# Sample top-k of a hybrid decoder step: one row of 1056 scores, or four quarter rows merged

## The chip, the cores and the metric

The kernel runs on one core of one Trainium2 chip as one program. The metric is device time in microseconds from start to end. Of five engines, TensorE (PE) multiplies, VectorE (DVE) and ScalarE (ACT) work on vectors, GpSimd (POOL) does side work and SyncE (SP) issues most DMAs. All wait for each other by semaphores.

## The reference

A two-layer decoder trunk processes 256 prompt tokens and 32 sample tokens (8 sequences of 4) with shared weights. Layer 0 has, between two SwiGLU halves, a sparse attention beside RWKV-7. The sample part of that attention is what changes; its definition, cut:

```python
def dsa_sample(q, k, v, qi, ki, wi, ck, cv, cki, page_table):
    ki_all = jnp.concatenate([ki_past, ki], axis=1)          # 1024 past keys from 8 pages, then the new ones
    isc = indexer_scores(qi, ki_all, wi)                     # sum over 16 heads of relu(qi . ki) * wi
    isc = jnp.where(adm[None], isc, -jnp.inf)
    vals, sel = lax.top_k(isc, topk)                         # topk = 256
    ...
    kg = jnp.where(is_past, ck[phys, off].astype(k.dtype), gather_rows(k, new_i))
    vg = jnp.where(is_past, cv[phys, off].astype(v.dtype), gather_rows(v, new_i))
    return sparse_attend(q, kg, vg, jnp.isfinite(vals))      # softmax over the 256 chosen keys
```

The prompt part is the same with 256 keys and the best 64 of them. The kernel does not gather: it turns the choice into a mask of 0 and -1e30 and adds it to dense scores.

## The kernel before, in words

Everything around the change is `dsa_stage`, in the profile from 364 to about 569 us. The rest of the program (four feed-forward stages, projections, RWKV, retention and mLSTM) stands as it is, and starts after this stage ends on all engines.

Each engine has its own list of instructions, in the order in which the code is written; semaphores set who waits.

- SP loads parameters (L1351), then the cache pages by the page table: `load` (L1353) reads eight page numbers into registers and issues eight DMAs of 256 KB. Keys of sequences 0 and 1 go first, those of 2 and 3 once `is_sum` is 12 (the index keys are read), then values of 0 and 1, keys of 4 to 7, values of 2 to 7. Each later load waits until TensorE is done with the slot (`kv_used`).
- Index scores: for the prompt L1395, L1547 and L1620. For the samples TensorE runs 12 steps (4 groups of two sequences by 3 chunks of 512, 512 and 32 keys): a product with the index keys (L1419), a ReLU on ACT (L1554), and `weigh` (L1407), which sums the heads into 32 rows in banks 5 to 7.
- VectorE picks the prompt's top 64 (L1631, L1635), copies the sample scores into `iss` and `wks` (L1666 to L1670, 32 rows of 1056), then goes through the eight prompt heads. `head(h)` (L1650, L1651) takes the row maximum, which ACT's exponential (L1570) waits for; `norm(h)` (L1656) gives the reciprocal sum to ACT; `out` (L1660) stores a pair of heads. Between two heads stand four calls of `top_eight` (L1676, L1678): take the eight largest of each of the 32 rows, and strike them out. 32 calls give 256.
- TensorE for each head h: scores (L1474 product, L1476 adds the prompt's mask), transposes of head h-1 (L1434, waits for ACT's norm, which stands after the exponential of head h), values of head h-2 (L1445), and after each odd head the dense key scores of two sequences (L1462).
- After the last head VectorE makes the mask (L1692, L1693; semaphore `ms_done`), TensorE spreads it (L1495), and softmax, transposes (L1505) and values (L1524, L1526) of the samples follow.

```python
for i in range(h * (KS // 8) // 8, (h + 1) * (KS // 8) // 8):
    top_eight(i)
```

## Time and profile before

| | |
|---|---|
| three timed runs | 1709.56, 1713.64 (median), 1715.57 us |
| profiled execution | 1715.16 us, span of the core 1713.3 us |
| busy in the span | PE 1516.6 (89%), DVE 1158.1 (68%), ACT 311.5 (18%), POOL 304.1 (18%) us |
| DMA | 232.77 MB, mean 136 GB/s |

How to read it: busy shares are averages over stages with different limits; the changed stage is about an eighth of the span and is read from its own rows. The profile follows the chain that ended last only through the final stages, so the path through this stage is put together here from the timelines of VectorE, TensorE and SP and from who waited for whom.

### The profile page before, as it was taken

To read this page: it belongs to the slowest core of one execution; us is meant where nothing else is said; L and a number is where in the kernel's file an instruction comes from. 1 tells how busy PE (TensorE), PEld (TensorE's weight loads), DVE (VectorE), ACT (ScalarE), POOL (GpSimd) and SP (SyncE) were. 2 spreads that over 40 slices of the span, in tenths; PEclk is the share of its full clock that TensorE was granted. 3 is DMA by queue.
4 is the path that set the end of the run, shared out by engine and by line. 5 is a ranking of instruction groups with operands and counts; after the bars stand their busy time and mean duration, and the time that the engine had idled before them with its cause. 6 is when DMAs were issued, how large, how long until landed. Compare 5 with 4: busy or idle time off the path is not lost. (4 is left out here: it accounts for less than half of the span.)

```text
span 1713.3 us, 28197 instructions
## 1 busy us (share of the span) xinstructions
PE 1516.6 (89%) x11288; PEld 1346.1 (79%) x11288; DVE 1158.1 (68%) x1396; ACT 311.5 (18%) x599; POOL 304.1 (18%) x270
## 2 busy tenths in 40 slices
PE   6999999986778568668999989999998986999997
PEld 6999989952333258468999989999895664899997
DVE  6877857639782473478876868768573447687764
ACT  2111020022111222123111021110201202321110
POOL 3333120000000000024332133321100000343310
PEclk9999999987768779879999999999999566999999
DMA  7442716533745200044443634426142003444242
GB/s 272 148 171 90 243 47 217 196 109 130 240 148 175 74 1 3 29 175 190 169 171 117 217 110 172 168 89 240 67 159 99 5 25 126 166 172 171 98 135 96
DMA packets 62963, 232.77 MB, mean 136 GB/s; under 512 B 9271, under 2 KB 19165, under 8 KB 45717
## 3 DMA queue, kind: packets, MB, share of 16 engines
q1 hardware_dynamic: 51578, 225.81, 37.4%
q10 hardware_dynamic: 11290, 5.63, 1.1%
q8 instruction: 68, 1.11, 0.3%
q14 instruction: 27, 0.21, 0.0%
HBM read 225.31 MB, written 6.10 MB: 135 GB/s over the span
## 5 line engine op out<-in xcount | busy, mean ns | idle before, releaser
L185 PE MATMUL psum<-x_hi_r,pair_hi 128*128 128x288 f32 x1744 | 520.7, 299 | 36.0 <-DVE ring_r L180 36.0
L187 PE MATMUL psum<-x_hi_r,ring_r 128*128 128x288 f32 x1744 | 519.5, 298 | 0.0
L186 PE MATMUL psum<-x_lo_r,pair_hi 128*128 128x288 f32 x1616 | 478.7, 296 | 0.0
L185 PEld LDWEIGHTS psum<-x_hi_r,pair_hi 128*128 128x128 f32 x1744 | 332.4, 191 | 39.5 <-DVE ring_r L180 39.1
L187 PEld LDWEIGHTS psum<-x_hi_r,ring_r 128*128 128x128 f32 x1744 | 331.8, 190 | 0.0
L180 DVE TENSOR_TENSOR ring_r<-ring,pair_hi 128x2048 fp32r<-128x2048 f32 x127 | 327.2, 2577 | 4.3
L186 PEld LDWEIGHTS psum<-x_lo_r,pair_hi 128*128 128x128 f32 x1616 | 306.4, 190 | 0.4
L185 PE MATMUL psum<-hidden_hi_r,down_hi 128*128 128x288 f32 x704 | 208.5, 296 | 0.0
L186 PE MATMUL psum<-hidden_r,down_hi 128*128 128x288 f32 x704 | 207.9, 295 | 0.0
L187 PE MATMUL psum<-hidden_hi_r,down_r 128*128 128x288 f32 x704 | 207.2, 294 | 0.0
L171 DVE CAST pair_hi<-ring 128x2048 fp32r<-128x2048 f32 x127 | 159.4, 1255 | 34.7 <-DMA ring<-in_w_gu 17.3
L614 POOL TENSOR_TENSOR hidden<-silu,up 128x288 f32 x88 | 128.4, 1459 | 148.9 <-ACT silu L543 147.3
L187 PEld LDWEIGHTS psum<-hidden_hi_r,down_r 128*128 128x128 f32 x704 | 132.6, 188 | 0.0
L186 PEld LDWEIGHTS psum<-hidden_r,down_hi 128*128 128x128 f32 x704 | 132.2, 188 | 0.0
L185 PEld LDWEIGHTS psum<-hidden_hi_r,down_hi 128*128 128x128 f32 x704 | 132.0, 188 | 0.0
L180 DVE TENSOR_TENSOR down_r<-down,down_hi 128x1408 fp32r<-128x1408 f32 x64 | 116.6, 1822 | 2.2
L543 ACT ACTIVATE silu<-gate 128x288 f32<-128x288 f32 x88 | 39.2, 446 | 425.5 <-DVE gate L558 425.5
L180 POOL TENSOR_TENSOR hidden_r<-hidden,hidden_hi_r x88 | 74.1, 842 | 212.5 <-DVE hidden_hi_r L171 212.5
L558 DVE TENSOR_TENSOR gate<-psum,rstd 128x288 f32<-128x288 f32 x88 | 40.0, 455 | 95.4 <-PE psum L187 95.3
L171 DVE CAST down_hi<-down 128x1408 fp32r<-128x1408 f32 x64 | 62.1, 970 | 49.3 <-PE psum L187 29.0
L229 PE MATMUL psum<-x_hi_r,pair_hi 128*128 128x288 f32 x192 | 54.5, 304 | 17.4 <-DVE ring_r L180 12.0
L622 POOL TENSOR_TENSOR ysq<-ysq,y 128x288 f32<-128x288 f32 x24 | 30.6, 1277 | 181.0 <-ACT y L549 181.0
(488 smaller groups left out, 1930.0 us busy)
## 6 DMA issues: line engine op xcount, KB each, us to landing
ring<-in_w_gu SPq DMA_DIRECT2D x88, 1024.0 KB, 4.8
down<-in_w_down SPq DMA_DIRECT2D x64, 704.0 KB, 4.4
ring<-in_w_ab SPq DMA_DIRECT2D x18, 1024.0 KB, 5.2
ring<-in_w_cd SPq DMA_DIRECT2D x13, 1024.0 KB, 4.8
ring<-in_cache_k SPq DMA_DIRECT2D x32, 256.0 KB, 4.2
index_keys<-in_cache_k SPq DMA_DIRECT2D x32, 256.0 KB, 4.1
index_keys<-in_cache_i ACTq DMA_DIRECT2D x64, 64.0 KB, 2.7
eight_pages_ds<-in_cache_v SPq DMA_DIRECT2D x16, 256.0 KB, 4.3
```

Of the source, the lines that this page charges most:

```text
L171: return dve.tensor_copy(hi, a)
L180: return eng.tensor_tensor(lo, a, hi.bitcast(F32), ALU.subtract)
L185: pe.matmul(out, w_hi, x_hi, start=start, stop=False)
L186: pe.matmul(out, w_hi, x_lo, start=False, stop=False)
L187: return pe.matmul(out, w_lo, x_hi, start=False, stop=stop)
L229: pe.matmul(out, c.whi[:, s, half, k], c.xhi[:, k], start=(k == 0), stop=False)
L543: act.activation(silu[:, b], gate[:, b], ACT.Silu).then_inc(silu_done, 1)
L558: dve.tensor_tensor(gate[:, b], c.banks[bank][:, 0:NT], c.rstd[:, :], ALU.mult).then_inc(gate_scaled, 1)
L614: pool.tensor_tensor(h, silu[:, b], up[:, b], ALU.mult).then_inc(c.hidden_raw, 1)
L622: pool.tensor_tensor(ysq[:, :], ysq[:, :], y2[:, n % 2], ALU.add).then_inc(ysq_added, 1)
```

## The change

The 1056 scores of each sample row are cut into four quarters of 264 (256 past keys and 8 of the 32 new ones), and the quarters stand below each other in 128 partitions. `weigh` writes them so into one bank. `wq` is the copy on which the rounds run; quarters 1 and 3 are multiplied by -1 through a column of ±1 beside the mask (`nmask[:, 8:9]`), so their rounds bring up the smallest of the original values. 33 rounds of `top_eight` write a sorted row of 264 into `sq`. POOL issues DMAs that bring the scores back into `iss` (32 rows of 1056) and a sorted quarter beside its neighbour. `merge_quarters` takes the 256 largest of quarters 0 and 1, and of 2 and 3, and sorts them by eight levels of pairwise maximum and minimum; one more DMA puts the second list beside the first, and `select` finds the 256th value, marks what is above it, and of the equal ones as many as are missing, in order. The rounds are spread over the heads by `ROUNDS` as 6, 6, 5, 5, 6, 5, 0, 0. A second parameter tile `nmask32` is loaded, and SP queues the values of sequence 1 right behind the keys of sequences 0 and 1.

```diff
+QW = KS + 8
+ROUNDS = (0, 6, 12, 17, 22, 28, 33, 33, 33)
...
-        iss, wks = sb("iss", [NS, KEYS]), sb("wks", [NS, KEYS])
-        t8s = sb("t8s", [NS, 8])
+        iss, rank = sb("iss", [NS, KEYS]), sb("rank", [NS, KEYS])
+        above = ymix[0:NS, 4:8].rearrange("p a t -> p (a t)")[:, 0:KEYS]
+        quarters = z[:, 10:16].rearrange("p a t -> p (a t)")
+        iq, wq, sq = (quarters[:, i * QW:(i + 1) * QW] for i in range(3))
+        moved, pa_, pb_ = (quarters[:, 3 * QW + i * KS:3 * QW + (i + 1) * KS] for i in range(3))
+        n_above, n_equal, kth = (sb(n, [NS, 1]) for n in ("n_above", "n_equal", "kth"))
...
             for b in range(2):
                 load("cache_k", b, KEY_SLOTS[b], None)
+            load("cache_v", 1, VALUE_SLOTS[1], None)
             for b in range(2, 4):
                 load("cache_k", b, KEY_SLOTS[b], (S["is_sum"], 12))
-            for b in range(2):
-                load("cache_v", b, VALUE_SLOTS[b], (S["is_used"], 12) if b == 0 else None)
+            load("cache_v", 0, VALUE_SLOTS[0], (S["is_used"], 12))
             for b in range(4, NB):
                 load("cache_k", b, KEY_SLOTS[b], (S["kv_used"], b // 2 - 1))
             for b in range(2, NB):
...
+            pool.wait_ge(S["is_out"], 2)
+            for s in range(4):
+                pool.dma_start(iss[:, s * KS:(s + 1) * KS], iq[quarter(s), 0:KS]).then_inc(S["q_moved"], 16)
+                pool.dma_start(iss[:, PAST + s * 8:PAST + s * 8 + 8], iq[quarter(s), KS:QW]).then_inc(S["q_moved"], 16)
+            pool.wait_ge(S["ts_max"], QW // 8)
+            for s in (0, 2):
+                pool.dma_start(moved[quarter(s), :], sq[quarter(s + 1), 8:QW]).then_inc(S["q_moved"], 16)
+            pool.wait_ge(S["ts_max"], QW // 8 + 1)
+            pool.dma_start(moved[quarter(0), :], pa_[quarter(2), :]).then_inc(S["q_moved"], 16)
...
                 pe.wait_ge(S["is_rel"], n + 1)
-                pe.matmul(B[5 + ch][0:NS, 0:w], wsel[:, g], rel[:, n % 3, 0:w], start=(g == 0), stop=(g == 3)).then_inc(S["is_used"], 1)
+                if ch < 2:
+                    for e in range(2):
+                        mm = pe.matmul(B[5][quarter(2 * ch + e), 0:KS], wsel[:, g], rel[:, n % 3, e * KS:(e + 1) * KS],
+                                       start=(g == 0), stop=(g == 3), skip_group_check=True)
+                else:
+                    for s in range(4):
+                        mm = pe.matmul(B[5][quarter(s), KS:QW], wsel[:, g], rel[:, n % 3, 8 * s:8 * s + 8],
+                                       start=False, stop=(g == 3), skip_group_check=True)
+                mm.then_inc(S["is_used"], 1)
...
-            for ch, (c0, w) in enumerate(CHUNKS):
-                dve.wait_ge(S["is_used"], 10 + ch)
-                if ch < 2:
-                    dve.tensor_copy(iss[:, c0:c0 + w], B[5 + ch][0:NS, 0:w]).then_inc(S["is_out"], 1)
-                else:
-                    dve.tensor_tensor(iss[:, c0:c0 + w], B[5 + ch][0:NS, 0:w], nmask[:, :], ALU.add).then_inc(S["is_out"], 1)
-            dve.wait_ge(S["is_out"], 3)
-            ln(dve.tensor_copy(wks[:, :], iss[:, :]))
+            dve.wait_ge(S["is_used"], 12)
+            dve.wait_ge(S["mp_done"], 1)
+            dve.tensor_copy(iq[:, 0:KS], B[5][:, 0:KS]).then_inc(S["is_out"], 1)
+            dve.tensor_tensor(iq[:, KS:QW], B[5][:, KS:QW], nmask[:, 0:8], ALU.add).then_inc(S["is_out"], 1)
+            dve.wait_ge(S["is_out"], 2)
+            ln(dve.tensor_scalar(wq, iq, nmask[:, 8:9], None, ALU.mult))
 
             def top_eight(i):
 
                 if i:
                     dve.wait_ge(S["ts_rep"], i)
-                dve.max(t8s[:, :], wks[:, :]).then_inc(S["ts_max"], 1)
-                dve.wait_ge(S["ts_max"], i + 1)
-                dve.match_replace(out=wks[:, :], in_to_replace=t8s[:, :], in_values=wks[:, :], imm_value=TAKEN).then_inc(S["ts_rep"], 1)
+                dve.max(sq[:, 8 * i:8 * i + 8], wq).then_inc(S["ts_max"], 1)
+                if i < QW // 8 - 1:
+                    dve.wait_ge(S["ts_max"], i + 1)
+                    dve.match_replace(out=wq, in_to_replace=sq[:, 8 * i:8 * i + 8], in_values=wq, imm_value=TAKEN).then_inc(S["ts_rep"], 1)
+
+            def merge_quarters():
+
+                dve.wait_ge(S["ts_max"], QW // 8)
+                dve.wait_ge(S["q_moved"], 160)
+                dve.scalar_tensor_tensor(pa_[quarter(0)], moved[quarter(0)], -1.0, sq[quarter(0), 0:KS], ALU.mult, ALU.max)
+                ln(dve.scalar_tensor_tensor(pa_[quarter(2)], sq[quarter(2), 0:KS], -1.0, moved[quarter(2)], ALU.mult, ALU.min))
+                a, b = pa_, pb_
+                d = KS // 2
+                while d >= 1:
+                    av, bv = (x.rearrange("p (m e d) -> p m e d", e=2, d=d) for x in (a, b))
+                    dve.tensor_tensor(bv[0:96, :, 0], av[0:96, :, 0], av[0:96, :, 1], ALU.max)
+                    last = dve.tensor_tensor(bv[0:96, :, 1], av[0:96, :, 0], av[0:96, :, 1], ALU.min)
+                    if d == 1:
+                        last.then_inc(S["ts_max"], 1)
+                    else:
+                        ln(last)
+                    a, b = b, a
+                    d //= 2
+
+            def select():
+
+                dve.wait_ge(S["q_moved"], 176)
+                ln(dve.scalar_tensor_tensor(pb_[quarter(0)], moved[quarter(0)], -1.0, pa_[quarter(0)], ALU.mult, ALU.max))
+                ln(dve.tensor_reduce(kth[:, :], pb_[quarter(0)], AX_X, ALU.min))
+                ln(dve.tensor_scalar(above, iss[:, :], kth[:, 0:1], None, ALU.is_gt))
+                dve.tensor_reduce(n_above[:, :], above, AX_X, ALU.add)
+                ln(dve.tensor_scalar(iss[:, :], iss[:, :], kth[:, 0:1], None, ALU.is_equal))
+                dve.tensor_scalar(n_equal[:, :], n_above[:, :], -1.0, float(KS), ALU.mult, ALU.add)
+                ln(dve.tensor_tensor_scan(rank[:, :], c.ones[0:NS, 0:1].to_broadcast([NS, KEYS]), iss[:, :], 0.0, ALU.mult, ALU.add))
+                ln(dve.scalar_tensor_tensor(rank[:, :], rank[:, :], n_equal[:, 0:1], iss[:, :], ALU.is_le, ALU.mult))
+                ln(dve.tensor_tensor(rank[:, :], rank[:, :], above, ALU.add))
+                ln(dve.tensor_scalar(iss[:, :], rank[:, :], -NEG, NEG, ALU.mult, ALU.add))
+                dve.tensor_tensor(iss[:, PAST:KEYS], iss[:, PAST:KEYS], nmask32[:, :], ALU.add).then_inc(S["ms_done"], 1)
 
             for h in range(8):
                 head(h)
@@ -1683,14 +1743,14 @@
                     norm(h - 1)
                 if h >= 4 and h % 2 == 0:
                     out(h // 2 - 2)
-                for i in range(h * (KS // 8) // 8, (h + 1) * (KS // 8) // 8):
+                for i in range(ROUNDS[h], ROUNDS[h + 1]):
                     top_eight(i)
+                if h == 6:
+                    merge_quarters()
             norm(7)
+            select()
             out(2)
             out(3)
-            dve.wait_ge(S["ts_rep"], KS // 8)
-            ln(dve.tensor_scalar(iss[:, :], wks[:, :], -2.0e38, NEG, ALU.is_gt, ALU.mult))
-            dve.tensor_tensor(iss[:, PAST:KEYS], iss[:, PAST:KEYS], nmask[:, :], ALU.add).then_inc(S["ms_done"], 1)
             for g in range(2):
```

VectorE before, from the last rounds behind the eighth head to the mask (`t8s_ds` holds the eight maxima, `wks_ds` the copy that is struck out; L1656 is `norm`, L1660 `out`):

```order
L1650 TENSOR_REDUCE mx_ds<-psum 128x2 [waits sp_sum_ds]
L1651 TENSOR_SCALAR nb_ds<-mx_ds 128x2 [waits chain_dve]
L1656 RECIPROCAL ri_ds<-rs_ds 128x2 [waits sp_exp_ds]
L1676 MAX t8s_ds<-wks_ds 32x8 [waits ts_rep_ds]
L1678 MATCH_REPLACE wks_ds<-t8s_ds,wks_ds 32x1056 [waits ts_max_ds]
...
L1656 RECIPROCAL ri_ds<-rs_ds 128x2 [waits sp_exp_ds]
L1660 COPY ymix<-psum 128x256 [waits op_sum_ds] x2
L1692 TENSOR_SCALAR iss_ds<-wks_ds 32x1056 [waits ts_rep_ds]
L1693 TENSOR_TENSOR iss_ds<-iss_ds,nmask_ds 32x32 [waits chain_dve]
```

And after, the same place (L1677 and L1678 are `head`, L1683 `norm`, L1687 `out`, L1728 to L1738 `select`; `z` is the tile that now holds the quarters):

```order
L1677 TENSOR_REDUCE mx_ds<-psum 128x2 [waits sp_sum_ds]
L1678 TENSOR_SCALAR nb_ds<-mx_ds 128x2 [waits chain_dve]
L1683 RECIPROCAL ri_ds<-rs_ds 128x2 [waits sp_exp_ds] x2
L1728 SCALAR_TENSOR_TENSOR z<-z 32x256 [waits q_moved_ds]
L1729 TENSOR_REDUCE kth_ds<-z 32x1 [waits chain_dve]
L1730 TENSOR_SCALAR ymix<-iss_ds,kth_ds 32x1056 [waits chain_dve]
...
L1737 TENSOR_SCALAR iss_ds<-rank_ds 32x1056 [waits chain_dve]
L1738 TENSOR_TENSOR iss_ds<-iss_ds,nmask_ds 32x32 [waits chain_dve]
L1687 COPY ymix<-psum 128x256 [waits op_sum_ds] x2
```

The four rounds between the last two reciprocals are gone; the selection stands behind them and ahead of the last two stores, and waits for POOL's last DMA.

VectorE after, between the seventh head and the eighth (L1701 is the last maximum of `top_eight`, L1710 to L1717 `merge_quarters`):

```order
L1701 MAX z<-z 128x8 [waits ts_rep_ds]
L1677 TENSOR_REDUCE mx_ds<-psum 128x2 [waits sp_sum_ds]
L1678 TENSOR_SCALAR nb_ds<-mx_ds 128x2 [waits chain_dve]
L1683 RECIPROCAL ri_ds<-rs_ds 128x2 [waits sp_exp_ds]
L1687 COPY ymix<-psum 128x256 [waits op_sum_ds]
L1710 SCALAR_TENSOR_TENSOR z<-z 32x256 [waits q_moved_ds,ts_max_ds]
L1711 SCALAR_TENSOR_TENSOR z<-z 32x256
L1716 TENSOR_TENSOR z<-z 96x128 [waits chain_dve]
L1717 TENSOR_TENSOR z<-z 96x128
```

The last round ends ahead of the seventh head; the merge, of which the first of eight levels is shown, stands ahead of the eighth head's maximum and waits for POOL's first ten DMAs.

TensorE, the first steps of the sample index scores, before (L1419 is the product with the keys, L1407 `weigh`):

```order
L1419 MATMUL psum<-index_keys,qi_ds 64x512 x3
L1407 MATMUL psum<-down,wsel_ds 32x512 [waits is_rel_ds]
L1419 MATMUL psum<-z,qi_ds 64x32 x2
L1407 MATMUL psum<-down,wsel_ds 32x512 [waits is_rel_ds]
L1419 MATMUL psum<-index_keys,qi_ds 64x512 [waits is_rel_ds,index_keys_landed]
```

And after (L1446 the product, L1428 and L1432 `weigh`):

```order
L1446 MATMUL psum<-index_keys,qi_ds 64x512 x3
L1428 MATMUL psum<-down,wsel_ds 32x256 [waits is_rel_ds]
L1428 MATMUL psum<-down,wsel_ds 32x256
L1446 MATMUL psum<-z,qi_ds 64x32 x2
L1428 MATMUL psum<-down,wsel_ds 32x256 [waits is_rel_ds]
L1428 MATMUL psum<-down,wsel_ds 32x256
L1446 MATMUL psum<-index_keys,qi_ds 64x512 [waits is_rel_ds,index_keys_landed]
L1446 MATMUL psum<-index_keys,qi_ds 64x512
L1432 MATMUL psum<-down,wsel_ds 32x8 [waits is_rel_ds]
L1432 MATMUL psum<-down,wsel_ds 32x8 x3
```

Each product of 512 columns is now two of 256 that go to different column groups of 32, and each of 32 columns is four of 8.

## Rows read from the trace of the kernel before

**Rows 1.** Waits, 335 to 560 us: us in total, times, longest.
```profile
ACT x_hi L1570 <- DVE nb_ds L1651: 61.3, 8, 12.3
DVE mx_ds L1650 <- PE psum L1476: 13.2, 4, 4.9
```

**Rows 2.** Tiles t8s_ds, iss_ds: ns min/median/max, first, last start us.
```profile
L1676 DVE MAX8 t8s_ds<-wks_ds x32: 1227/1249/1249, 412.5 to 512.5; 32x8 f32<-32x1056 f32 x32
L1678 DVE MATCH_VALUE_LOAD wks_ds<-t8s_ds,wks_ds x32: 79/79/79, 413.8 to 513.8; 32x8 f32 x32
L1678 DVE MATCH_REPLACE8 wks_ds<-t8s_ds,wks_ds x32: 1229/1230/1232, 413.9 to 513.9; 32x1056 f32<-32x1056 f32 x32
...
L1692 DVE TENSOR_SCALAR iss_ds<-wks_ds x1: 686/686/686, 520.2 to 520.2; 32x1056 f32<-32x1056 f32 x1
```

**Rows 3.** Timeline of VectorE: start us, us, engine, line, [idle before].
```profile
411.74 0.69 DVE L1650 TENSOR_REDUCE mx_ds<-psum 128x2 f32<-128x512 f32 x1 [0.63 <-PE psum L1476]
...
422.93 0.67 DVE L1650 TENSOR_REDUCE mx_ds<-psum 128x2 f32<-128x512 f32 x1
...
437.29 0.69 DVE L1650 TENSOR_REDUCE mx_ds<-psum 128x2 f32<-128x512 f32 x1 [3.06 <-PE psum L1476]
...
492.23 0.69 DVE L1650 TENSOR_REDUCE mx_ds<-psum 128x2 f32<-128x512 f32 x1 [4.64 <-PE psum L1476]
...
503.82 0.67 DVE L1650 TENSOR_REDUCE mx_ds<-psum 128x2 f32<-128x512 f32 x1
```

**Rows 4.** VectorE's groups by line and shape: busy us, mean ns | idle before.
```profile
L1620 DVE SCALAR_TENSOR_TENSOR ymix<-down,wip_ds,ymix 128x256 f32<-128x256 f32 x32 | 15.4, 484 | 3.6 <-ACT down L1547 1.6
...
L1635 DVE MATCH_REPLACE8 z<-t_ds,z 128x256 f32<-128x256 f32 x16 | 6.4, 407 | 0.0
...
L1631 DVE MAX8 t_ds<-z 128x8 f32<-128x256 f32 x16 | 5.9, 412 | 0.0
...
L880 DVE TENSOR_TENSOR_SCAN D_rk<-seg_rk,D_rk 128x288 f32<-128x288 f32 x4 | 2.7, 737 | 0.0
...
L1701 DVE TENSOR_REDUCE mxs_ds<-down 128x1 f32<-128x1056 f32 x2 | 2.5, 1253 | 0.1
```

**Rows 5.** Timeline of TensorE: start us, us, engine, line, [idle before].
```profile
402.80 1.05 PE L1407 MATMUL psum<-down,wsel_ds 128*32 128x512 f32 x2
...
409.44 1.13 PE L1474 MATMUL psum<-z 64*128 64x256 f32 x4
...
499.97 2.07 PE L1476 MATMUL psum<-z,ident 128*128 128x256 f32 x4
...
509.53 7.71 PE L1462 MATMUL psum<-index_keys,qz_ds 128*32 128x512 f32 x32
...
518.01 1.84 PE L1445 MATMUL psum<-x_hi,vtok 128*64 128x256 f32 x8
...
521.18 2.38 PE L1495 MATMUL psum<-iss_ds,bsel_ds 32*128 32x512 f32 x6 [1.33 <-DVE iss_ds L1693]
...
542.68 7.06 PE L1524 MATMUL psum<-ring,x_lo 128*32 128x512 f32 x32
```

**Rows 6.** Stretches of TensorE: us, busy (x), granted clock, DMA share, GB/s.
```profile
496.00:502.00 6.00, 6.00 (x13) 0.50 0.70 236
510.00:518.00 8.00, 8.00 (x52) 0.94 0.00 0
```

**Rows 7.** Waits of the DMA queue SP, 335 to 560 us, as rows 1.
```profile
SPq L1359 <- PE psum L1462: 20.5, 3, 10.2
SPq L1359 <- PE psum L1419: 19.2, 1, 19.2
```

**Rows 8.** Timeline of the DMA queue SP: start us, us, line, DMAs issued.
```profile
429.44 0.85 SPq L1359 DMA_DIRECT2D two_pages_ds<-in_cache_v  x2
435.26 3.95 SPq L1359 DMA_DIRECT2D eight_pages_ds<-in_cache_v  x8
```

More of the change, by code:

```diff
@@ L1284, in dsa_stage @@
         "ip_sum", "ip_rel", "ip_acc", "is_sum", "is_rel", "is_used", "is_out",
-        "tp_max", "tp_rep", "mp_done", "ts_max", "ts_rep", "ms_done",
+        "tp_max", "tp_rep", "mp_done", "q_moved", "ts_max", "ts_rep", "ms_done",
         "sp_sum", "ri_done", "nb_done", "sp_exp", "pn_done", "pt_sum", "pt_out", "op_sum", "op_out",
@@ L1294, in dsa_stage @@
         cmask = sb("cmask", [P, 2, TP])
-        nmask = sb("nmask", [NS, NS])
+        nmask, nmask32 = sb("nmask", [P, 9]), sb("nmask32", [NS, NS])
         esel = sb("esel", [16, P])
@@ L1345, in half, with quarter @@
             return slice(u * 64, u * 64 + 64)
+        def quarter(s):
+            return slice(s * NS, s * NS + NS)
         @block.sync
         def _(sp):
-            for dst, src in ((kidg[:, :], "kidg"), (cmask[:, :, :], "cmask"), (nmask[:, :], "nmask"), (esel[:, :], "esel"),
+            for dst, src in ((kidg[:, :], "kidg"), (cmask[:, :, :], "cmask"), (nmask[:, :], "nmask"), (nmask32[:, :], "nmask32"), (esel[:, :], "esel"),
                              (wmask[:, :, :], "wmask"), (bsel[:, :, :], "bsel")):
@@ L1383, in _ @@
             pe.matmul(B[0][:, 0:NT], c.half_ones[:, :], kisq[:, :], start=True, stop=True).then_inc(S["ki_sum"], 1)
-            pe.wait_ge(S["par_loaded"], 96)
+            pe.wait_ge(S["par_loaded"], 112)
             for t in range(2):
@@ L1451, in key_scores @@
                     pe.wait_ge(S["qz_done"], 1)
-                    pe.wait_ge(S["is_out"], 3)
+                    pe.wait_ge(S["is_out"], 2)
                 if b0 == 4:
@@ L1598, in ln @@
                 c.link(dve, "dve", ins)
-            dve.wait_ge(S["par_loaded"], 96)
+            dve.wait_ge(S["par_loaded"], 112)
             dve.wait_ge(S["ki_sd"], 1)
@@ L2449, in lay_out_dsa @@
     t, s = np.arange(NS)[:, None], np.arange(NS)[None]
-    m["nmask"] = np.where((s <= t) & (s // TS == t // TS), 0, NEG).astype(np.float32)
+    m["nmask32"] = np.where((s <= t) & (s // TS == t // TS), 0, NEG).astype(np.float32)
+    m["nmask"] = np.concatenate([m["nmask32"].reshape(NS, 4, 8).transpose(1, 0, 2).reshape(P, 8), 1.0 - 2.0 * (np.arange(P)[:, None] // NS % 2)], 1).astype(np.float32)
     row = np.arange(P)
```

## The prediction, made before the changed kernel was run

> **What bounds the stage now.** I began with who waited for whom around the attention stage, because the profile's chain of waits covers only the end of the program. Two rows matter: ScalarE's exponentials waited 61.3 us in eight waits for VectorE's head maxima, and VectorE's head maxima waited 13.2 us in four for TensorE's scores [rows 1]. So VectorE is late at most heads, TensorE at some. The timeline of VectorE shows which [rows 3]. From head 0 (411.74) to head 1 (422.93) it has no idle time: 11.19 us, almost all of it top-k rounds. Head 2 comes at 437.29 after 3.06 us idle, so there TensorE is last. From head 6 (492.23, after 4.64 idle) to head 7 (503.82) are 11.59 us without idle again. The pattern alternates: the steps 0-1, 2-3, 4-5 and 6-7 are VectorE's, the steps 1-2, 3-4 and 5-6, which hold the dense key scores, are TensorE's.
>
> I then asked in each VectorE step when TensorE would have been ready. For head 7 its mask product starts at 499.97 and takes 2.07, so it ends at 502.04 [rows 5]; the head starts at 503.82 [rows 3]. That small difference is the point of this forecast: TensorE stands close behind VectorE.
>
> **Cost of a round.** Before, 32 rounds of 1.249 + 0.079 + 1.230 = 2.56 us by their medians [rows 2]; with the gaps, about 0.07 in the step from head 0 to 1 ((11.19 - 0.80 for the head's own work) / 4 = 2.60), I take 2.62, 84 us in all. After, 33 rounds of 264 elements. The same two operations with 256 elements took 0.412 and 0.407 [rows 4]; between 256 and 1056 elements the slope is 1.04 ns an element, so 264 give 0.42 and 0.415. With the value load 0.08 and the gaps 0.07 a round is 0.985 us, 33 are 32.5 us. VectorE thus gets rid of about 52 us, but the time falls only by what TensorE lets through:
>
> 1. *Weighing of the sample scores.* A product of 512 columns took 1.05 us in two passes, 0.52 a pass [rows 5]. Where neighbouring products go to other column groups, 32 passes of 512 took 7.06, 0.22 each [rows 5]. The change makes two products of 256 columns in different column groups of each of eight such ones: four passes of half the length, 4 x 0.11 = 0.44, say 0.55. That saves 0.45 to 0.5 each, 3.9 in all; the four small products become four of 8 columns each, +0.1 each. So TensorE starts head 0's scores 3.4 earlier than at 409.44 [rows 5], less 0.5 for the added parameter load ahead of the stage (eight DMA issues took 3.95, 0.49 each [rows 8]), on which both engines wait. VectorE copies 264 columns instead of 1056 meanwhile, under these scores. It is itself busy with the prompt's top-k until about 407, which holds the gain at about **3.0**. Bounds: 3.4 if nothing binds; -0.7 (a loss) if the passes do not overlap and the added ones cost 0.2 us.
> 2. *Head 0 to 1.* TensorE has these scores early. VectorE needs 0.8 + 6 x 0.985 = 6.7 instead of 11.19: **4.5**. Bounds of a round 0.9 and 1.1 give 5.0 and 3.8.
> 3. *Heads 2-3, 4-5 and 6-7.* VectorE would need 7.3 (head, reciprocal, store and six rounds, or the merge), TensorE 502.1 - 492.23 = 9.9. So 11.59 becomes 9.9: 1.7 each, three times **5.1**. TensorE is late next.
> 4. *Heads 1-2, 3-4, 5-6.* TensorE's already, with VectorE idle: **0**.
> 5. *Merge.* Two operations of 256 at 0.484 [rows 4]; eight levels of two of 128 elements, each 0.484 less 128 x 1.04 ns = 0.35, plus 0.07 for the link: 1.0 + 6.2 = 7.1 us, from 1.5 us after head 6 to 8.6. Hidden by TensorE's 9.9; if strided access doubled the levels, head 7 would be 4.9 late.
> 6. *End.* The mask product started at 521.18, after 1.33 idle, while the last values ended at 518.01 + 1.84 = 519.85 [rows 5]. With the mask ready earlier it starts then: **1.3**. The mask must be ready: `select` begins at head 7 + 1.9 and has one operation of 256 (0.48), a reduction of 256 (0.42 by the slope from 1253 [rows 4]), three scalar passes of 1056 at 0.686 [rows 2], three more of at most 1.25, a scan of 1056 elements (288 took 0.737 [rows 4]: 2.7), three small ones and nine gaps, 1.2: 10.6 us, so it ends at head 7 + 12.5. The `out` copy behind it is needed by values 6 at 518.01 - 503.82 = head 7 + 14.2. Hidden with 1.3 to spare.
> 7. *Values of sequence 1 earlier.* The load takes about 9 us of SP (5.0 for the page numbers between 430.29 and 435.26, 3.95 to issue [rows 8]) and moves into a wait of 19.2 us for the last index-key product [rows 7]. The keys of sequences 4 and 5 can then be issued 9 us earlier, but SP waited 20.5 us in three waits for TensorE's key scores anyway [rows 7], and no key score waited for pages in this trace. **0**, from -0.5 to 1.
> 8. *POOL's eleven DMAs.* POOL had nothing else there. The first ten have until the merge, some 10 us after the last round. The eleventh must land by head 7 + 14.2 - 0.4 - 10.6 = head 7 + 3.2, that is 13.1 after head 6, and is released at 8.6: 4.5 us. Page loads of 256 KB share the DMA engines; this one is 32 KB. **0**, at worst 3 to 4 us.
>
> All behind the mask (softmax, transposes, values, last pages) follows TensorE's steps as before and only moves. Sum: 3.0 + 4.5 + 5.1 + 1.3 = 13.9 us. The profiled execution took 1715.16; 1715.16 - 13.9 = 1701.3. It was 1.5 above the median 1713.64 of the runs, so I forecast 1713.64 - 13.9 = 1699.7, said as **1700**. What can be told from no change is 0.3%, 5.1 us.
>
> **Rivals.**
> *TensorE's clock stays up (1692).* In 496 to 502 TensorE was busy all 6.00 us at a granted clock of 0.50, its level of 1.2 GHz, after waiting; in 510 to 518, key scores, it had 0.94, nearly 2.4 GHz [rows 6]. After the change its wait ahead of each odd head's transposes is 1.7 us shorter (item 3). If that keeps 2.4 GHz, a VectorE step needs 6.9 on TensorE and 7.3 on VectorE: 2.6 more, three times, 8 us. Against it: the other wait, for ScalarE's result behind each even head, stays as it is, and the stretch at 0.50 stands behind that one.
>
> *TensorE's clock does not come back (slower).* Its place is the four blocks of key scores. One took 7.71 us [rows 5], at 0.94; the same work at 0.50 takes 14.5, so 6.8 more. Four such blocks cost 27 us: 1699.7 + 27 = 1727. It decides from the third block on (two cost 13.6, the gain). Against it: the clock came up in this block after a longer wait than it will have now.
>
> *Weighing does not overlap.* Then item 1 gives -0.7 instead of 3.0: 1703.4. The 0.22 of a pass speaks against it; there both neighbours have their own data in SBUF, here they share weights.
>
> *POOL's transfers are late.* A last DMA that takes L us after its release costs L - 4.5: at 8 us 1703, at 14 us 1709. The rows for it are missing: POOL issues no DMA in this stage before. The Trainium skill, "SBUF — State Buffer", section "SBUF: two separate sides", says that a DMA issued from GpSimd cannot have its descriptors written while VectorE runs an operation in a two-port mode, and its next section tells of 620 ns becoming 3100. By that rule 2.5 us would be added, still inside the 4.5, so the sum would stay at 1700; no row here shows it. VectorE is idle behind the merge, so there is little to hold POOL up.
>
> *The steps hide nothing new (no change).* If TensorE's chain grew by what VectorE gives up in items 2, 3 and 6, for instance by page loads in its way, 1709 to 1714 would be left. No key score waited for pages, so little speaks for it.
>
> **How the numbers follow.** Forecast 1700 (its own range 1696 to 1704): 0.58. Clock stays up: 0.14. No overlap in weighing: 0.10. POOL late: 0.09, of which 0.02 ends within 0.3%. No change: 0.05. Slower by the clock: 0.04. Faster by over 0.3% (below 1708.5): 0.58 + 0.14 + 0.10 + 0.07 = 0.89; same 0.07; slower 0.04. The range from 1689 to 1708 takes in the clock rival and the two small losses and leaves out the last two and the far end of the first.
>
> **What would show it.** Right: rounds of about 0.98 us; 6.7 us from head 0 to 1 and 9.9 from 2 to 3, 4 to 5 and 6 to 7, each with VectorE now waiting for TensorE's scores (L1503); head 0 about 3 us earlier; merge of 7 and selection of 11 us or less, followed by no wait on TensorE; the mask product right behind the last values. Wrong: a head that waits for POOL's DMAs; a clock of 1.0 between even and odd heads, or of 0.5 in the key scores; products of 256 columns that take 0.5 us each; a mask product that waits for `select`.

## The result, and the profile after

The changed kernel took **1683.8 us** (median of 4 runs, 1682.84 to 1693.94) against 1713.7: ratio 0.984, 95% interval 0.980 to 0.988. That is 29.9 us faster where 13.9 were forecast, and outside the range of 1689 to 1708. Run twice more beside the experiments it gave 1689.0 and 1685.0; over all 14 of its runs the median is 1685.9, over all 67 of the kernel before 1713.3, so the change is worth about 27 us. Its profiled execution had a span of 1681.1 (before: 1713.3), its mean granted clock was 0.928 (before: 0.912).

All stretches below are read from the traces. "Start to head 0" runs from the stage's first product of the index keys' sums to VectorE's first head maximum, "end" from head 7 to the mask product (L1495 before, L1522 after), the last row from POOL's first memset of the RWKV stage to POOL's first copy behind it, in the output projection; all in us:

| stretch | before | after | change | forecast |
|---|---|---|---|---|
| start to head 0 | 47.07 | 43.53 | -3.5 | -3.0 |
| head 0-1 | 11.19 | 6.68 | -4.5 | -4.5 |
| 2-3, 4-5, 6-7 | 11.26, 11.59, 11.59 | 7.96, 7.07, 7.96 | -11.4 | -5.1 |
| 1-2, 3-4, 5-6 | 14.36, 16.15, 15.94 | 14.81, 13.86, 15.49 | -2.3 | 0 |
| end | 17.36 | 14.14 | -3.2 | -1.3 |
| RWKV stage behind it (unchanged code) | 175.75 | 169.32 | -6.4 | 0 |

The rest of the program gives -0.8, the whole -32.2. The timeline of VectorE in the changed kernel (start us, us, engine, line, idle before it and its releaser), where [rows 3] stood:

```profile
407.12 0.69 DVE L1677 TENSOR_REDUCE mx_ds<-psum 128x2 f32<-128x512 f32 x1 [0.29 <-PE psum L1503]
...
413.80 0.68 DVE L1677 TENSOR_REDUCE mx_ds<-psum 128x2 f32<-128x512 f32 x1
...
428.61 0.69 DVE L1677 TENSOR_REDUCE mx_ds<-psum 128x2 f32<-128x512 f32 x1 [8.00 <-PE psum L1503]
...
436.57 0.69 DVE L1677 TENSOR_REDUCE mx_ds<-psum 128x2 f32<-128x512 f32 x1 [2.14 <-PE psum L1503]
...
450.43 0.69 DVE L1677 TENSOR_REDUCE mx_ds<-psum 128x2 f32<-128x512 f32 x1 [8.03 <-PE psum L1503]
...
457.50 0.68 DVE L1677 TENSOR_REDUCE mx_ds<-psum 128x2 f32<-128x512 f32 x1
```

VectorE waits for scores at six heads now instead of four, and not at head 5 (457.50), where it was still forecast to wait. The waits of the stage, where [rows 1] stood, say the same (us in total, times, longest):

```profile
ACT x_hi L1597 <- DVE nb_ds L1678: 45.9, 8, 12.3
...
DVE mx_ds L1677 <- PE psum L1503: 30.4, 6, 10.2
```

The rounds, from the tile view (ns min/median/max, first and last start), where [rows 2] stood:

```profile
L1701 DVE MAX8 z<-z x33: 414/436/436, 407.9 to 462.3; 128x8 f32<-128x264 f32 x33
...
L1704 DVE MATCH_VALUE_LOAD z<-z x32: 92/92/93, 408.4 to 461.8; 128x8 f32 x32
L1704 DVE MATCH_REPLACE8 z<-z x32: 416/417/419, 408.5 to 461.9; 128x264 f32<-128x264 f32 x32
...
L1716 DVE TENSOR_TENSOR z<-z x8: 286/286/290, 475.1 to 478.7; 96x128 f32<-96x128 f32 x8
```

0.436 + 0.092 + 0.417 and the gaps make a round of 1.00 us (MAX8 at 407.92, the next at 408.92), against 0.985 forecast. Merge and selection, again VectorE's timeline:

```profile
474.19 0.40 DVE L1710 SCALAR_TENSOR_TENSOR z<-z 32x256 f32<-32x256 f32 x1
...
478.94 0.28 DVE L1717 TENSOR_TENSOR z<-z 96x128 f32<-96x128 f32 x1
480.95 0.69 DVE L1677 TENSOR_REDUCE mx_ds<-psum 128x2 f32<-128x512 f32 x1 [1.73 <-PE psum L1503]
...
483.01 0.39 DVE L1728 SCALAR_TENSOR_TENSOR z<-z 32x256 f32<-32x256 f32 x1
...
492.43 0.18 DVE L1738 TENSOR_TENSOR iss_ds<-iss_ds,nmask_ds 32x32 f32<-32x32 f32 x1
```

The merge is over 1.73 us before head 7, the selection takes 9.6 us and is over 2.4 us before TensorE has finished the last values (at 495.00). Now TensorE's timeline, where [rows 5] stood. It is here that the trace departs from the forecast:

```profile
393.59 0.63 PE L1428 MATMUL psum<-down,wsel_ds 128*32 128x256 f32 x4
...
431.40 1.11 PE L1461 MATMUL psum<-ident,x_hi 128*128 128x128 f32 x4 [2.83 <-ACT x_hi L1591]
432.44 1.97 PE L1472 MATMUL psum<-x_hi,vtok 128*64 128x256 f32 x4
434.34 1.13 PE L1501 MATMUL psum<-z 64*128 64x256 f32 x4
435.40 1.13 PE L1503 MATMUL psum<-z,ident 128*128 128x256 f32 x4
...
439.36 0.66 PE L1461 MATMUL psum<-ident,x_hi 128*128 128x128 f32 x4 [2.83 <-ACT x_hi L1591]
439.95 1.08 PE L1472 MATMUL psum<-x_hi,vtok 128*64 128x256 f32 x4
440.96 7.06 PE L1489 MATMUL psum<-index_keys,qz_ds 128*32 128x512 f32 x32
...
493.17 1.83 PE L1472 MATMUL psum<-x_hi,vtok 128*64 128x256 f32 x8
495.09 2.35 PE L1522 MATMUL psum<-iss_ds,bsel_ds 32*128 32x512 f32 x6
```

Behind head 2 (431.40) the four transposes take 1.11 us and the four products of the values 1.97, the speed of 1.2 GHz. The scores of head 3 behind them (L1501, L1503) take 1.13 each, the speed of 2.4 GHz, where such a product took 2.07 in the step that the forecast used [rows 5]. That alone makes head 3 some 2 us earlier. Behind head 3 (439.36), after a wait of the same 2.83 us, transposes and values take 0.66 and 1.08: 2.4 GHz, which stays through the key scores. The stretches (us, busy, granted clock, DMA share, GB/s) put the clock beside it, where [rows 6] stood:

```profile
430.00:437.00 7.00, 5.13 (x16) 0.76 0.74 221
437.00:444.00 7.00, 4.64 (x24) 1.00 0.69 231
444.00:451.00 7.00, 6.39 (x44) 1.00 0.63 223
```

POOL's DMAs, from the view of DMA issues (KB each, median us from issue to landing), and POOL's timeline:

```profile
iss_ds<-z POOLq DMA_DIRECT2D x4, 32.0 KB, 5.0
z<-z POOLq DMA_DIRECT2D x3, 32.0 KB, 2.5
```

```profile
479.51 0.50 POOL L1397 DMA_DIRECT2D z<-z  x1 [15.46 <-DVE z L1717]
```

Nothing waited for them.

### The profile page after: what moved, and what is told of

It is laid out like the page before. It is cut to its first block and busy times, and to the rows that moved or that the text cites. A ratio compares the mean times of both kernels' runs of the same rounds, so it can differ in the third digit from the quotient of the medians.

```text
span 1681.1 us, 28318 instructions
## 1 busy us (share of the span) xinstructions
PE 1494.1 (89%) x11328; PEld 1337.2 (80%) x11328; DVE 1117.7 (66%) x1423; ACT 310.8 (18%) x599; POOL 309.0 (18%) x281
## 3 DMA queue, kind: packets, MB, share of 16 engines
q8 instruction: 68, 1.11, 0.3%
```

## The experiments

Twelve runs were made: eight further kernels, the changed kernel twice more, and e2 and the kernel before once more each. The theory under test: the part that the forecast missed is TensorE's clock, not work. Rival theories: the earlier loads of values did it; or the changed kernel's stage merely came at a lucky moment.

**Both ends of the clock taken away.** To the changed kernel, small products whose results are never read were added where TensorE waits for ScalarE (behind `mm.then_inc(S["sp_sum"], 1)`), so that it idles less; the kernel before got the same with 24, 12 or 5 of them:

```diff
+for _ in range(0 if h == 0 else 14 if h == 1 else 5 if h % 2 else 5):
+    pe.matmul(B[2 if h < 2 else (h + 1) % 2][:, 0:TP], c.ident[:, :], mp[:, 0], start=True, stop=True, skip_group_check=True)
```

> The changed kernel with products whose result nobody reads (identity by a prompt mask tile, 128x256), issued by TensorE behind the scores of each head from the second on: 14 behind head 1's, 5 behind each later one, so that it is busy where it would wait. Theory A: the remaining stretches at 1.2 GHz go: 1-2 13.4 instead of 14.8 us, 2-3 and 6-7 about 7.1 instead of 8.0, 5-6 13.9 instead of 15.5: 4 to 5 us less than the changed kernel, near 1679. Theory B: the products do not make anything faster, 1684 or a few us more where they delay the transposes.

> The kernel before with the same kind of unread products: 24 behind head 1's scores, 12 behind later odd heads', 5 behind even ones'. VectorE's rounds stay as long as before. Theory A: VectorE's steps stay at 11.2 to 11.6 us, but 3-4 and 5-6 fall from 16.1 to about 13.9 and 1-2 from 14.4 to 13.4, about 5 to 6 us less in all (1708). Theory B: no change, 1713.7, or slower.

e2: 1682.87 us (1681.24 to 1685.35); e3: 1706.12 (1704.19 to 1715.09), ratio to before 0.996, 0.994 to 0.998. In the traces the stretch from head 0 to the mask product is 81.64 us in e2 and 103.06 in e3, against 87.97 and 109.44 without filling. So filling is worth 6.4 us in the kernel before, and 6.3 against this trace of the changed one. With the clock up in both the change takes 21.4 us from this stretch: 4.5 in step 0-1, 14.1 in the steps 2-3, 4-5 and 6-7, 2.8 at the end, and nothing in the other steps. Without filling it was 21.5 in this trace, but 14.9 and 19.3 in two later ones (e5, e10); that 21.5 and 21.4 agree is chance. The forecast for this stretch, 10.9 us, set the new work against the old clock. In time, e2 is only 1 us below the first runs of the changed kernel and 3 below all 14: its RWKV stage came out longer (174.71 against 169.32), on which more below.

**One part at a time.** e1: the kernel before, with rounds over the first 264 scores only; it leaves the other three quarters out of the choice, and nothing else moved. e8: the kernel before with only the weighing in quarters; it copies the first quarter four times and so leaves the other three out as well.

```diff
-dve.max(t8s[:, :], wks[:, :]).then_inc(S["ts_max"], 1)
+dve.max(t8s[:, :], wks[:, 0:264]).then_inc(S["ts_max"], 1)
...
-dve.match_replace(out=wks[:, :], in_to_replace=t8s[:, :], in_values=wks[:, :], imm_value=TAKEN).then_inc(S["ts_rep"], 1)
+dve.match_replace(out=wks[:, 0:264], in_to_replace=t8s[:, :], in_values=wks[:, 0:264], imm_value=TAKEN).then_inc(S["ts_rep"], 1)
```

> The kernel before, with one edit: the 32 rounds read and strike only the first 264 of the 1056 scores (the other three quarters of the scores are left out of the choice). It has no quartered weighing, no merge, no selection, no moves by POOL and the old order of loads, so it isolates the length of the rounds. Theory A (TensorE's clock stays up once its waits for VectorE are short): 0-1 takes 4.9 us, 2-3 and 6-7 about 8.0, 4-5 7.1 to 8, 3-4 13.9 instead of 16.15, the end 15.4; from head 0 to the mask product 88 us against 109.4 before, about 21 us faster in that stretch. Theory B (only the VectorE steps shrink and TensorE's own speed stays as it was): 0-1 4.9, the three other VectorE steps 9.9, TensorE's steps 14.4 to 16.1 as before: about 11 us faster.

e1: 1699.45 (1698.04 to 1701.42), ratio 0.990, 0.987 to 0.993: 14 us, half of the whole. Head 0 to mask 95.61, between the 88 of theory A and the 98.4 of theory B, so neither was met. Its trace shows what is missing. After the second wait of 2.83 us its clock was still at 1.2 GHz, and the key scores began there (TensorE's timeline):

```profile
441.81 1.12 PE L1434 MATMUL psum<-ident,x_hi 128*128 128x128 f32 x4 [2.83 <-ACT x_hi L1564]
442.86 1.97 PE L1445 MATMUL psum<-x_hi,vtok 128*64 128x256 f32 x4
444.76 7.82 PE L1462 MATMUL psum<-index_keys,qz_ds 128*32 128x512 f32 x32
```

For e8 the products of `weigh` are those of the change, and `iss` is filled from them:

```diff
+dve.wait_ge(S["is_used"], 12)
+for c0 in (0, 256, 512, 768):
+    dve.tensor_copy(iss[:, c0:c0 + 256], B[5][0:NS, 0:256])
...
```

> The kernel before with only the quartered weighing: two products of 256 columns, or four of 8, in different column groups of one bank. VectorE copies the first quarter of the scores four times instead of all four quarters (three quarters of the scores are left out). If the passes overlap, the last weighing ends about 3.5 us earlier and head 0 comes 2.3 us earlier than before: about 1711. If they do not, head 0 comes 0.5 us later than before. The steps from head 0 on as before, 11.2, 14.4, 11.3, 16.1, 11.6, 15.9, 11.6.

e8: 1713.66 (1704.13 to 1716.37), ratio 0.9993, 0.998 to 1.001: no gain. Head 0 came 2.4 us earlier, so the halves do overlap, but steps 1-2 and 3-4 took 15.47 and 16.71 instead of 14.36 and 16.15, because the key scores ran more of their time at the lower clock. The first block of them, TensorE's timeline:

```profile
423.37 1.11 PE L1447 MATMUL psum<-ident,x_hi 128*128 128x128 f32 x4 [12.96 <-ACT x_hi L1577]
424.41 9.25 PE L1475 MATMUL psum<-ring,qz_ds 128*32 128x512 f32 x32
```

32 products in 9.25 us, where the same block took 8.14 in the kernel before and such a block takes 7.06 at the full clock. A gain ahead of a wait can be lost to the clock behind it.

**Is it the length of the waits?** e4 gives the changed kernel its long steps back: VectorE has six more reductions at heads 2, 4 and 6.

```diff
+if h in (2, 4, 6):
+    for _ in range(6):
+        ln(dve.tensor_reduce(t8[:, 0, 0:1], cmask[:, :, :].rearrange("p a t -> p (a t)"), AX_X, ALU.max))
```

> The changed kernel with six reductions of 128x512 that nobody reads behind the rounds of heads 2, 4 and 6 (behind the merge at head 6), 0.72 us each, 4.3 a head: VectorE's steps 2-3, 4-5, 6-7 take 10.3 to 11.4 us again and TensorE waits as long as before. Theory A: TensorE's clock falls again: 3-4 goes back from 13.9 to 16.1, the end from 14.1 to about 16, beside the 2.4, 4.3 and 2.7 us of the lengthened steps: 13 to 14 us slower than the changed kernel, near 1697. Theory B: only the lengthened steps, 9.4 us, near 1693, and 3-4 stays at 13.9.

e4: 1702.55 (1698.78 to 1704.39), ratio 0.992, 0.989 to 0.995. Head 0 to mask 103.13, 15.2 more than in the changed kernel's trace; the lengthened steps themselves hold 8.9 of that (10.05, 11.39, 10.46 instead of 7.96, 7.07, 7.96), the other 6.3 lie in steps 3-4 and 5-6 and the end, whose work is unchanged. Against e5 and e10 that second part is 3.4 and 5.6. e5, below, lost as much with nothing lengthened, so e4 fits the theory without proving it; and of the waits behind the odd heads it made only one much longer (3.04, 6.22 and 3.45 us, where the kernel before had 4.22, 4.54 and 4.54). Its transposes and values run at 1.2 GHz behind every head from 2 on:

```profile
469.28 1.11 PE L1461 MATMUL psum<-ident,x_hi 128*128 128x128 f32 x4 [6.22 <-ACT x_hi L1591]
470.32 1.97 PE L1472 MATMUL psum<-x_hi,vtok 128*64 128x256 f32 x4
472.22 8.22 PE L1489 MATMUL psum<-ring,qz_ds 128*32 128x512 f32 x32
```

**Is it the moment?** The changed kernel twice more, and once with its prompt top-k, and with it the heads, some 2 us later:

```diff
+for _ in range(3):
+    ln(dve.tensor_reduce(mx[:, 0, 0:1], cmask[:, :, :].rearrange("p a t -> p (a t)"), AX_X, ALU.max))
```

> The changed kernel once more, unchanged, for a second trace and more times. Theory A (how fast TensorE's clock comes and goes depends on the lengths of its waits alone): the steps from head 0 on repeat to 0.1 us (6.68, 14.81, 7.96, 13.86, 7.07, 15.49, 7.96, end 14.14) and the RWKV stage repeats 169.3. Theory C (after waits of 2.8 us the clock falls or stays by where in time they lie, so that it differs between executions): the even-odd steps lie between 6.7 and 10, the odd-even ones between 13.8 and 16.8, their sum differs by several us, and the RWKV stage lies somewhere between 169 and 176.

> The changed kernel with three reductions of 128x512 that nobody reads ahead of the prompt's top-k, so that everything from head 0 on comes about 2.1 us later and nothing behind is changed. Theory A: all steps as in the changed kernel, 2.1 us slower (about 1686). Theory C: the steps come out otherwise, with stretches at 1.2 GHz in other heads, and the time changes by something else than 2.1 us, anywhere from -3 to +10.

> The changed kernel unchanged, a third trace and more times beside the filled one. Theory C: head 0 to the mask product between 82 and 99 us, the steps that differ from the other two traces are those with stretches at 1.2 GHz; steps 0-1 and 4-5 (VectorE's) at 6.7 and 7.1 always. Median of its runs between 1684 and 1690.

e5: 1688.96 (1683.75 to 1689.6), ratio 0.984, 0.982 to 0.987; e10: 1685.03 (1683.36 to 1691.61); e6: 1684.47 (1683.12 to 1691.31), not to be told from them. Head 0 to mask in the traces: 94.59 in e5, 90.11 in e10, 87.95 in e6. The same program, then, with waits of the same length, keeps the clock at one head and loses it at another. In e5, behind head 3, where the first trace had 0.66 and 1.08:

```profile
441.25 1.12 PE L1461 MATMUL psum<-ident,x_hi 128*128 128x128 f32 x4 [2.83 <-ACT x_hi L1591]
442.30 1.97 PE L1472 MATMUL psum<-x_hi,vtok 128*64 128x256 f32 x4
444.20 7.19 PE L1489 MATMUL psum<-index_keys,qz_ds 128*32 128x512 f32 x32
```

```profile
430.00:437.00 7.00, 5.60 (x14) 0.56 0.72 233
437.00:444.00 7.00, 4.17 (x12) 0.50 0.61 214
444.00:451.00 7.00, 7.00 (x33) 0.96 0.45 158
```

This execution did in steps 2-3 and 6-7 (9.85 us each) just what was forecast (9.9), and in 4-5 (7.07) not. The shift of e6 left the pattern of the first trace as it was, step by step within 0.02 us. It was a small test: head 0 came 2.1 us later within the stage, but the stage itself began earlier, so that it lay only 0.5 us later in the program (407.62 against 407.12).

**The filled kernel and the kernel before again**, to see which of the two repeats.

> The changed kernel with the unread products again, for a second trace. Theory C says that what differs between executions of the changed kernel is TensorE's clock after waits of 2.8 us; with the waits filled nothing is left to differ: head 0 to the mask product 81.6 us again within 0.3 (the changed kernel had 88.0 and 94.6 in two traces). Rival: something else differs between executions (DMA, chance of the chip), then it varies by several us here as well. Time: 2 to 6 us below the changed kernel of this call, less clear than in the stretch, because the RWKV stage (169 to 176 us) is not filled.

> The kernel before, a second trace. If its waits of 4 us and more always bring the clock down, its steps repeat within 0.6 us (11.2, 14.4, 11.3, 16.1, 11.6, 15.9, 11.6, end 17.4; 109.4 in all) and the stretch differs by less than 2 us, where the changed kernel's differed by 6.6. If the clock can stay up there too, the steps 1-2, 3-4 and 5-6 fall below 15 us in this trace. The RWKV stage tells whether its 175.7 against 169.3 of the changed kernel was chance: then it can be anything from 169 to 176 here.

e9: 1680.8 (1678.05 to 1685.17), ratio 0.981, 0.979 to 0.982; e11: 1712.61 (1709.54 to 1716.05). Head 0 to mask: 81.65 (e2: 81.64) and 109.56 (before: 109.44). The two ends repeat; what lies between them wanders over 6.6 us (87.97, 94.59, 90.11). In e9 the clock is 1.00 all through:

```profile
430.00:437.00 7.00, 6.33 (x31) 1.00 0.74 227
437.00:444.00 7.00, 7.00 (x33) 1.00 0.72 243
444.00:451.00 7.00, 6.33 (x45) 1.00 0.63 203
```

**The loads.** e7: the changed kernel with the load loop of before.

```diff
-load("cache_v", 1, VALUE_SLOTS[1], None)
...
-load("cache_v", 0, VALUE_SLOTS[0], (S["is_used"], 12))
+for b in range(2):
+    load("cache_v", b, VALUE_SLOTS[b], (S["is_used"], 12) if b == 0 else None)
```

> The changed kernel with the order of page loads of before (values of sequence 1 behind those of sequence 0). My forecast had 0 for this part: same as the changed kernel within 1 us apart from the clock. Rival: the early load is what took waits off the key scores, then key scores of sequences 4 and 5 would wait for pages here and it would be 2 us or more slower.

e7: 1692.46 (1686.25 to 1693.18), ratio 0.987, 0.984 to 0.989, beside e5 with 1688.96 and 1685.9 over all runs of the changed kernel. The intervals of the ratios overlap with those of e5. In the trace the stretch that the loads serve is the same, 88.16 against 87.97 in the first trace; what is longer is the RWKV stage behind it, 176.35 against 169.3 to 169.8 in the three traces of the changed kernel and in that of e6. The new loads do not prevent it: e2 and e9 have them and took 174.71 and 175.97 there. Whether the old ones make it more frequent is open, and with it up to 6.6 us of the total that the forecast put at nothing for this item.

**The RWKV stage's clock.** Its code is the same in all kernels. A window of TensorE some 14 to 20 us behind the stage's first memset (572.24 before, 545.67 after); first the kernel before, then the changed one:

```profile
586.00:592.00 6.00, 6.00 (x17) 0.50 0.00 0
```

```profile
559.00:565.00 6.00, 4.97 (x20) 0.86 0.00 0
```

TensorE works at 0.50 before and mostly at full clock after, on the same code. All traces fall into two groups by the moment at which the granted clock fell from 1.0 to 0.5 at the start of this stage. In the four with the short stage (the changed kernel, e5, e6, e10) it fell 1.3 to 1.9 us behind the memset and was back 15.0 to 15.6 us behind it, and the stage took 169.3 to 169.8. In the nine others with its waits unfilled it fell between 0.1 us ahead of the memset and 0.9 behind it, was back 20.4 to 21.4 us behind it, and the stage took 172.2 to 176.4. The nine are the kernel before and e11, all edits of it (e1, e3, e8), and e2, e4, e7 and e9. So less than half a microsecond in that moment goes with a full clock that comes back 5 us later; why the second group itself spreads over 4 us stays open. e12 is e2 with such products in three waits of this stage too:

```diff
+for _ in range(16):
+    pe.matmul(B[7][:, 0:NT], c.ident[:, :], c.x[:, 0], start=True, stop=True)
...
+for _ in range(13):
+    pe.matmul(B[5][:, 0:NT], c.ident[:, :], c.x[:, 0], start=True, stop=True)
...
+for _ in range(13):
+    pe.matmul(B[3][:, 0:NT], c.ident[:, :], c.x[:, 0], start=True, stop=True)
```

> The filled changed kernel with unread products (identity by a tile of x, 288 columns) in the RWKV stage too: 16 at its start, where TensorE waits 12.7 us for VectorE and ScalarE, 13 ahead of the second wait for VectorE (7.2 us) and 13 ahead of the third (7.1 us). Theory C, applied to this stage: its clock too comes up sooner or later in different executions (169.3 us in one trace of the changed kernel, 174.7 and 176.0 in the filled one), and with the first waits filled it starts at 2.4 GHz: the stage takes 169 us or less, the total about 7 to 10 us less than the filled kernel's 1681, near 1673; head 0 to the mask product stays 81.6. Rival: the 6 us of the RWKV stage have another cause than the clock: then it stays between 169 and 176, and the total near 1681 or above, since the products stand in the way.

e12: **1672.97** (1670.81 to 1677.57), ratio 0.977, 0.974 to 0.979, the fastest of all: 12.9 us below the changed kernel's 1685.9 and 8.3 below the filled one (1681.3 over the nine runs of e2 and e9). Head 0 to mask is again 81.64, the RWKV stage 165.87. Its windows about the same place (memset at 540.47):

```profile
552.00:558.00 6.00, 6.00 (x22) 0.72 0.00 0
558.00:564.00 6.00, 4.36 (x18) 1.00 0.01 3
```

## Why the prediction was wrong, point by point

1. *Weighing, 3.0:* right. 3.5, 3.3 and 3.2 us in the three traces of the changed kernel; a product of 512 in two passes took 1.05 us [rows 5], two column groups with four passes of 256 in all take 0.63, both also between 395 and 405 us, where the granted clock was 1.00. Head 0's scores started 3.7 us earlier behind the first index-key product (16.1 instead of 19.8), against 3.4 forecast; the half microsecond for the added parameter load is not told apart from chance (a wait of 3.36 and 3.77 us in two traces, 3.25 and 3.02 before). The Trainium skill, "TensorE: Matmul & The Clock Gate", section "Part 3: Packing small matmuls — row/col tiling", says that products in different tiles of the array run at the same time; the trace agrees, with 0.63.
2. *Head 0 to 1, 4.5:* right, 4.5 in every trace.
3. *Heads 2-3, 4-5, 6-7, 5.1:* **the step that failed.** It priced TensorE's part of the step at the 9.9 us of the trace before, in which its work ran at 0.50 [rows 6], and took that as a floor. Measured were savings of 11.4, 7.7 and 10.0 us in the three traces, and 14.1 with the waits filled in both kernels (e3 to e2). A step costs 9.85 where the clock is down, which is what was forecast, and 6.6 to 8.0 where it is back or never fell, near the 7.3 that VectorE was given in the rival. The prediction's own sign of being wrong, a clock of 1.0 between even and odd heads, was there (437 to 444). With the clock held up (e2) the steps 2-3 and 6-7 are 6.61 and 4-5 is 7.07.
4. *Heads 1-2, 3-4, 5-6, 0:* the cause, TensorE's own work, was right; the size followed the clock. 2.3, 0.9 and 1.6 us in the three traces. In the first it is all in 3-4 (13.86 against 16.15), where the key scores take 7.06 instead of 8.03 and the values 1.08 instead of 1.97; in e10 it is in 5-6 (13.86), and 3-4 was longer than before (16.79).
5. *Merge hidden:* right. It took 5.0 us instead of 7.1, because a level took 0.53 us and not 0.77: an operation of 96x128 took 0.286 and not 0.35, and the second of a level started 0.21 us after the first; it was over 6.2 us behind head 6 (8.6 forecast).
6. *End, 1.3:* the mask is in time and the product stands right behind the values, as forecast; 3.2, 1.7 and 3.2 us measured, the surplus again the clock on the last scores and values.
7. *Values of sequence 1, 0:* right for this stretch (e7: 0.2 us); the RWKV stage stays open, above.
8. *POOL's DMAs, 0:* right. The last was issued at 479.51; with 2.5 us it has landed by 482.5, and `select` starts at 483.01 without a wait. The moves of the scores, issued while VectorE ran its rounds, took 5.0 us, the three later ones, issued while it was idle, 2.5. The first group also ran among page loads, and no run separates the two, so the rule weighed in the prediction is neither borne out nor refuted.

The rival "TensorE's clock stays up" (1692, chance 0.14) was the right mechanism in the wrong place of the list. It was argued away with "the other wait, for ScalarE's result behind each even head, stays as it is, and the stretch at 0.50 stands behind that one". True of the first half: in the first trace the clock is indeed down behind heads 2 and 6 (431.40 with 1.11). But the forecast also took what lies behind that stretch, the odd head's products and the next key scores, at the clock of before, where the wait at the odd head was 1.3 to 1.7 us longer (4.22, 4.54 and 4.54 against 2.83, 3.28 and 2.83). TensorE's timeline of the kernel before has it there:

```profile
506.59 1.12 PE L1434 MATMUL psum<-ident,x_hi 128*128 128x128 f32 x4 [4.54 <-ACT x_hi L1564]
507.63 1.97 PE L1445 MATMUL psum<-x_hi,vtok 128*64 128x256 f32 x4
```

In the three traces of the changed kernel it was up again by the odd head, or had never fallen, at three, one and two of the three places. This rival's 13 us for the three steps is close to the 14.1 of the filled kernels; it gave the faster key scores and values behind them nothing. That it is the clock is shown (e3: 6.4 us less with no other change than filled waits; e2, e9 and e12: the changed kernel's stretch at 81.6 each time, where it wandered from 88.0 to 94.6 without filling). What the shorter waits themselves do to the clock is shown less well (e4, above). Why a wait of 2.83 us is followed by either clock in the same program is not: length alone does not decide it, and the small shift that was tried did not change it.

Two small slips in the prediction's working change nothing of this: it started all three steps at 11.59 us, but 2-3 took 11.26, so item 3 should have read about 4.8; and the gaps of a round are 2.60 - 2.56 = 0.04 us, not 0.07.

Of the 32.2 us between the two profiled executions the forecast's own items hold 13.9, the rest of the stage 11.1 (25.0 less 13.9), nearly all of it the clock, the clock in the RWKV stage, which was not in the forecast at all, 6.4. That last part is not shown to belong to the change: traces of the kernel before gave 175.75 and 172.24 there, filled ones 174.71 and 175.97, the changed one 169.3 to 169.7. It comes with a full clock 6 us earlier behind the memset, which goes with the moment at which the clock had fallen. All three traces of the changed kernel lie in the early group and both of the kernel before in the late one; what makes that so stays open. "Clock doesn't come back", "no overlap in weighing", "POOL late" and "no change" did not happen; the nearest to the first is e8, where the early start cost 2 us in the key scores.

## What to carry to other kernels

Before taking an engine's duration from a trace as its floor, look at the granted clock of that stretch: work at 0.50 between two waits can take half the time when the waits shrink, so price such a step at both clocks and let both be in the range, together with the stretches behind it. When VectorE's share of a pipeline shrinks, TensorE can gain twice, once from waiting less and once from running faster, and the second gain wanders from run to run until the waits are filled. Filling waits of TensorE with products that nobody reads made no step longer where ScalarE or VectorE is awaited anyway, and was worth 13 us here in both stages together. In the attention stage alone it was worth 4.6 us of time (1681.3 against 1685.9), less than the 6 to 13 us that its stretch gained, because the unfilled RWKV stage behind it took 5 to 7 us longer in both traces: look at the stage behind, too.

## What the runs showed of the hardware

- In the attention stage waits of 2.83 us were followed by TensorE at 2.4 GHz in one place and at 1.2 GHz in another, in one and the same execution (431.40 and 439.36) and at the same place in two executions of one program (439.36: 0.66; 441.25: 1.12). Head 0 to mask took 87.97, 94.59 and 90.11 us for it, and 81.64, 81.65 and 81.64 in the filled ones.
- Being busy was not enough to bring the clock back at once: 586 to 592 has TensorE busy for all 6.00 us at 0.50 before the change. The Trainium skill, "TensorE: Matmul & The Clock Gate", section "HAM oscillation — how this bites in real kernels", tells of a loop that swings between the two clocks with every wait and advises to restructure it so that TensorE stays busy; the traces agree with the swing, and e12 shows that idle products do for it where the loop can't be restructured (13 us of 1686).
- A round of eight on VectorE goes by the length of a row and hardly by its partitions: 128x264 took 0.436 + 0.092 + 0.417 us, 32x264 (e1) 0.424 + 0.079 + 0.404, and 32x1056 took 1.249 + 0.079 + 1.230. Cutting rows of 1056 into four and stacking them makes a round 2.6 times shorter (1.00 against 2.60 us with the gaps).
- A scan of 32x1056 elements took 2.33 us (2.7 estimated).
